# Moving every on-chip buffer of a two-block transformer kernel by 96 bytes, and packing the first block's split activations in 1,024-byte tiles

## The chip, the cores and the metric

The kernel runs on one NeuronCore of one Trainium2 chip. The metric is the device time of one execution in microseconds. TensorE (PE) multiplies, VectorE (DVE), ScalarE (ACT) and GpSimd (POOL) do the elementwise work, and DMA queues, nearly all of them issued by SyncE (SP), bring the weights from HBM.

## The reference

Two transformer blocks in float32, one after the other, on 256 tokens of width 2048 (the second one with 16 further meta tokens, so 272 positions). Each block is: norm, a wide input projection, two kinds of attention, an output projection, a residual, a norm, a gated MLP with 5632 hidden columns, a residual.

```
h = rms_norm(x, g_attn_pre) * (1 + scale_a) + shift_a
proj = h @ w_in                                   # 2048 x 5456
mixed = concat(diff_out, dsa_out) @ w_o           # 2048 x 2048
x = x + gate_a * rms_norm(mixed, g_attn_post)
h = rms_norm(x, g_ffn_pre) * (1 + scale_f) + shift_f
ff = (silu(h @ w_gate) * (h @ w_up)) @ w_down     # 2048 x 5632, twice, and 5632 x 2048
x = x + gate_f * rms_norm(ff, g_ffn_post)
# second block, 272 positions: h @ w_in_2 (2048 x 3904), attention, @ w_out_2,
# conv_glu: (silu(conv3(h @ w_gate)) * (h @ w_up)) @ w_down, same sizes
```

## The kernel before

Activations lie transposed on the chip: a tile has 128 channels on the partitions and the positions along the free dimension, so 16 tiles hold the width of 2048. The matmul takes its operands as `float32r` (one pass over the columns, with reduced precision), and the kernel wins the precision back by splitting both operands into a high and a low part. The weights arrive by DMA in `raw` (four slots of 128 x 2048 values, 1 MB each: 4 row tiles of 512 columns). ACT rounds a slot into `w_hi` (line 933), DVE subtracts that from the raw values into `w_lo` (line 1456); there are two buffers of each. PE then issues, for each of 4 output tiles and each of 4 row tiles, three matmuls: high by high, low by high, high by low.

```
pe.matmul(out, wh[:, k, c], hi(k0 + k), start=a0, stop=False)            # line 2108
pe.matmul(out, wh[:, k, c], lo(k0 + k), start=False, stop=False)         # line 2109
ins = pe.matmul(out, wl_[:, k, c], hi(k0 + k), start=False, stop=z)      # line 2110
```

The first operand is the stationary one (128 x 128 weights, loaded by a LDWEIGHTS of its own beside the matmul before), the second one moves (128 partitions by so many positions). One slot of weights gives 48 such matmuls. The order of the work is written out by hand in each engine's program and kept by semaphores.

The moving operands come from two pairs of buffers. `x_hi` and `x_lo` hold the split activations of width 2048, 16 tiles each. They are declared for 272 positions, so a tile takes 4 x 272 = 1,088 bytes of a partition, and the first block, which has 256 positions, uses the first 1,024 bytes of each. `hid_hi` and `hid_lo` hold the split hidden activations of the MLP, 44 tiles of 256 positions, 1,024 bytes each. The stretches with these matmuls, as the profile has them:

- 44 to 322 us: first block's input projection, 43 units of 48 and 36 matmuls (`x_hi`, `x_lo`, 256 positions), together 2,064
- 432 to 533: output projection, 768 (256 positions)
- 562 to 1076: gate and up projections, 4,224 (256 positions)
- 1076 to 1320: down projection, 2,112 (`hid_hi`, `hid_lo`)
- 1358 to 1830: second block's projections, 1,776 with 272 positions, 768 with 258
- 1830 to 2340: gate with 258 positions, 2,112, and up with 256 positions, 2,112, from the tiles of 1,088 bytes
- 2340 to 2602: down projection, 2,112 (`hid_hi`, `hid_lo`)

Every buffer has a fixed address, given out by `place` in the order of the declarations, each rounded up to 32 bytes, from a first address of 2208. 2208 is 160 more than a multiple of 256. The buffers that lie ahead of the constants (`raw`, `w_hi`, `w_lo`, `x_res`, `x_hi`, `x_lo`, and the arena with `hid_hi` and `hid_lo`) all have sizes that are multiples of 1,024 bytes, so before the change each of them begins 160 bytes past a multiple of 256. Within `w_hi` and `w_lo` the row tiles are 2,048 bytes apart and the column tiles 512 bytes. Only in the last unit of each quarter of the first input projection are the row tiles 336 columns, 1,344 bytes, apart.

Of the kernel before, what the change touches and what calls it, by code (L numbers as in the profile page):

```python
# [22 lines left out]
F32R = mybir.dt.float32r  # L23
# [4 lines left out]
P = 128  # L28
D = 2048
KT = D // P  # L30
# [127 lines left out]
def in1_width(n):  # L158

    return PROJ1 - 10 * COLS if ORDER_IN1[n] == 10 else COLS  # L160
# [69 lines left out]
def program(nc, a):  # L230
    with ExitStack() as ctx:
# [1 line left out]
            return ctx.enter_context(nc.semaphore(name))  # L233


        cursor = [2208]

        def place(name, shape, dt=F32, at=None):
            size = 4 * int(np.prod(shape[1:]))
            if at is None:  # L240
                at, cursor[0] = cursor[0], (cursor[0] + size + 31) // 32 * 32
            return nc.alloc_sbuf_tensor_at(name, shape, dt, offset=at)
# [14 lines left out]
        x_hi = place("x_hi", [P, KT, N2], F32R)  # L257
        x_lo_at = cursor[0]
        x_lo = place("x_lo", [P, KT, N2], F32R)
        branch_f = place("branch_f", [P, KT, S], at=x_hi_at)  # L260
        xmeta = place("xmeta", [META, D], at=x_lo_at)
        arena = cursor[0]
# [178 lines left out]
        def one(rows=P):  # L441
# [8 lines left out]
        kpe = proj2[0:64, T2_KPE, :]  # L450
        kpg = proj2[0:64, T2_CQ, :]
        norm("attn_pre", S, D, [[x_res[:, t, 0:S] for t in range(KT)]],
             [(0, x_res[:, t, 0:S], gain[:, 0, t:t + 1], x_hi[:, t, 0:S], x_lo[:, t, 0:S],
               mod[:, SH_A + t:SH_A + t + 1]) for t in range(KT)], True, given=x_sum)
        norm("diff", S, P, [[dout[:, h, :]] for h in range(8)],
             [(h, dout[:, h, :], lamv[:, 7:8], x_hi[:, h, 0:S], x_lo[:, h, 0:S], None) for h in range(8)], True)
        norm("attn_post", S, D, [[branch_a[:, t, :] for t in range(KT)]],
             [(0, branch_a[:, t, :], gain[:, 1, t:t + 1], branch_a[:, t, :]) for t in range(KT)], False,
             branch_a_ssq, direct=4)
        norm("ffn_pre", S, D, [[x_res[:, t, 0:S] for t in range(KT)]],  # L460
             [(0, x_res[:, t, 0:S], gain[:, 0, t:t + 1], x_hi[:, t, 0:S], x_lo[:, t, 0:S],
               mod[:, SH_F + t:SH_F + t + 1]) for t in range(KT)], True, column=True)
        norm("ffn_post", S, D, [[branch_f[:, t, :] for t in range(KT)]],
             [(0, branch_f[:, t, :], gain[:, 1, t:t + 1], branch_f[:, t, :]) for t in range(KT)], False,
# [32 lines left out]
        def out_bank(g):  # L497

            if g < 8:
                return bank[3]  # L500
            return bank[1 if g % 2 else 3] if g < 16 else bank[4 * (g % 2) + 3]
# [417 lines left out]
        def _(act):  # L919
# [245 lines left out]
            def take_out(g):  # L1165
                act.wait_ge(h_out, g + 1)
                b, h = out_bank(g), g % 8
                dst, src = {"diff": (dout[:, h, :], b[:, 0:S]), "dsa": (x_hi[:, 8 + h, 0:S], b[:, 0:S]),
                            "na": (na_out[:, h, 0:S], b[:, S:2 * S]),
                            "mla": (mla_out[:, h, 0:S], b[:, S:2 * S])}[kind(g)]  # L1170
                act.activation(dst, src, ACT.Copy).then_inc(h_taken, 1)
# [276 lines left out]
        def _(dve):  # L1448
# [326 lines left out]
            def take_low(g):  # L1775
                if kind(g) != "dsa":
                    return
                h = g - 8
                dve.wait_ge(h_taken, g + 1)
                dve.tensor_tensor(x_lo[:, 8 + h, 0:S], out_bank(g)[:, 0:S], x_hi[:, 8 + h, 0:S],  # L1780
                                  ALU.subtract).then_inc(h_low, 1)

            def heads(g0, g1, lead=None):
# [285 lines left out]
        def _(pe):  # L2069
# [11 lines left out]
            def dense(units, rows, hi, lo, n, cols=None, width=COLS, step=1, last_unit=True, base=0, ready=None,  # L2081
                      bank7=None, tile_ready=None, bank_ready=None, banks=None, lag=4):


                cols = cols or [P * m for m in range(len(rows))]
                for j, (k0, nk) in enumerate(units):
                    ps = d.at % SPLIT
                    if ready:
                        ready(j)
                    pe.wait_ge(raw_free[ur.at % RAW], ur.rounds())  # L2090
                    wh, wl_ = (w[ps][:, 0:nk * width].rearrange("p (k c) -> p k c", k=nk) for w in (w_hi, w_lo))
                    for m, r in enumerate(rows):
                        if j == 0:
                            free, c_ = (up_freed, up) if base else (bank_freed, t)
                            if lag == 4 or t.at + m >= lag:
                                pe.wait_ge(free, c_.value(m + 5 - lag))
                            if bank_ready:
                                bank_ready(m)
                            if bank7 is not None and m == 3:
                                pe.wait_ge(ada_copied, bank7)  # L2100
                        c = slice(cols[m], cols[m] + r)
                        out = (banks(m) if banks else bank[base + m])[0:r, 0:n]
                        for k in range(nk):
                            a0 = j == 0 and k == 0
                            if tile_ready and m == 0:
                                pe.wait_ge(n_lo, norms[tile_ready]["first"]["split"] + 4 * j + k + 1)
                            z = j == len(units) - 1 and k == nk - 1
                            pe.matmul(out, wh[:, k, c], hi(k0 + k), start=a0, stop=False)  # L2108
                            pe.matmul(out, wh[:, k, c], lo(k0 + k), start=False, stop=False)  # L2109
                            ins = pe.matmul(out, wl_[:, k, c], hi(k0 + k), start=False, stop=z)  # L2110
                        if j == len(units) - 1:
                            ins.then_inc(tile_done, 1 if m < len(rows) - 1 else 5 - len(rows))
                    if j < len(units) - 1:
                        ins.then_inc(split_used, 1)
                    if last_unit or j < len(units) - 1:
                        d.at += 1
                        ur.at += step(j) if callable(step) else step
                if base:
                    up.at += 4
                else:  # L2120
                    t.at += 4
# [2 lines left out]
                return (lambda k: x_hi[:, k, 0:n]), (lambda k: x_lo[:, k, 0:n])  # L2124


            pe.wait_ge(const_in, 16)
            pe.wait_ge(vec0_in, 48)
            pe.wait_ge(cleared, 1)
# [192 lines left out]
            for u in range(44):  # L2322
                part, n = divmod(u, 11)
                if u == 0:
                    pe.wait_ge(tile_done, 4)
                    pe.wait_ge(bank_freed, 4)
                if n == 0 and part:
                    pe.wait_ge(n_lo, norms["attn_pre"]["first"]["split"] + 4 * part + 4)
                if n in (0, 2, 4, 6):
                    ada_quarter(ADA_IN1 + 2 * part, n // 2)  # L2330
                ur.at = in1_unit(part, n)
                dense([K16[part]], TAIL1 if in1_width(n) < COLS else FOUR, *xs(S), S, width=in1_width(n),
                      banks=lambda m: in1_bank(u, m), lag=IN1_BANKS,
                      tile_ready=None if u else "attn_pre")
                if n == 6:
                    ada_columns(ADA_IN1 + 2 * part)
                if n == 7:
                    s = ADA_IN1 + 2 * part + 1
                    pe.wait_ge(beside_used, 4 * part + 4)
                    pe.wait_ge(ada_copied, s)  # L2340
                    for j in range(4):
                        ins = pe.matmul(bank[7][:, j:j + 1], acc_beside[:, P * j:P * j + P], one(), start=True,
                                        stop=True)
                    ins.then_inc(ada_cols, 1)
                if part == 3 and n in (5, 7, 8, 10):
                    rotate_rows({5: 0, 7: 1, 8: 2, 10: 3}[n])
                if u == 23:
                    pe.wait_ge(vec_in, 16 * VEC_LOADS)
                    for j in range(3):
                        ins = pe.transpose(bank[6][:, P * j:P * j + P], packs[:, 1 + j, :], ident)  # L2350
                    ins.then_inc(packs_turned, 1)
# [209 lines left out]
                    pe.wait_ge(n_lo, norms["diff"]["first"]["split"] + 4 * (j - 1))  # L2561

            def out1(i, ready=None, bank_ready=None):
                dense(K_O, FOUR, *xs(S), S, step=2, ready=ready, bank_ready=bank_ready)
                ada_sum(i + ADA_OUT1)
            pe.wait_ge(ada_copied, ADA_OUT1)
            ur.at = UNIT_OUT1
# [19 lines left out]
            spread("ffn_pre")  # L2587

            def mlp1(i, tile_ready=None, ada_block=None):
                dense(K16, FOUR, *xs(S), S, tile_ready=tile_ready,  # L2590
                      step=2 if ada_block is not None else (lambda j: 9 if j == 0 else 1) if tile_ready else 1)
                if ada_block is not None:
                    pe.wait_ge(up_freed, up.value(4))
                    ada_sum(ada_block, bank[7])
                dense(K16, FOUR, *xs(S), S, base=4, bank7=None if ada_block is None else ada_block + 1)
            mlp1(0, "ffn_pre")
            loop(4, (8, 4, 12, 4), lambda i: mlp1(i + 1, ada_block=i + ADA_MLP1))
            loop(6, (8, 4, 8, 4), lambda i: mlp1(i + 5))
# [209 lines left out]
```

## Time and profile before

| | |
|---|---|
| median of 3 runs | 2601.63 us (2600.87 to 2602.52) |
| profiled execution, first to last instruction | 2602.4 us |
| PE busy | 2494.1 us (96%), 20,022 matmuls |
| DVE, ACT, POOL busy | 1441.4, 1033.4, 292.1 us |
| DMA | 504 MB, 57% of the 16 engines' span in the main queue |

"Busy" of PE counts overlapping matmuls, each some 0.28 us long, while a new one starts every 0.12 us; so the pace is read from the starts, or from how many there are in a window. In a window's count stand also those that had begun ahead of it. Idle time of an engine is put down to what released it. The profile's own execution differs from the median of the runs by less than 1 us.

### The profile page before, as it was taken

The page shows a single profiled execution, that of the slowest core. Times are in us where ns is not written, and L with a number is a line of the kernel's source. Part 1 is how long each engine was busy: PE and PEld are TensorE (multiplying, and loading weights), DVE is VectorE, ACT ScalarE, POOL GpSimd, SP SyncE. Part 2 cuts the span into 40 slices and gives each one's busy share as a digit, 9 for nine tenths or more (in the row PEclk, how much of TensorE's full clock was granted, in tenths as well). Part 3 has the DMA queues.
Part 4 walks back from the last instruction along what each step waited for, and adds up shares of the span by engine and source line. Part 5 has one row for each costly group of instructions (what it writes and reads, how often), then busy time and mean ns, then how long its engine had stood idle before and what let it go on. Part 6 is the DMA issues. An engine that isn't in the chain of part 4 may idle for free.

```text
span 2602.4 us, 47889 instructions
## 1 busy us (share of the span) xinstructions
PE 2494.1 (96%) x20022; PEld 2363.1 (91%) x20022; DVE 1441.4 (55%) x1926; ACT 1033.4 (40%) x1332; POOL 292.1 (11%) x372
## 2 busy tenths in 40 slices
PE   6999988989999999999989998998999999999999
PEld 4999847969999999999979997778999999999999
DVE  3677657965674444433455555655655555554443
ACT  3533244344333343333334336443444444443333
POOL 5000122410100000011113002113000000000000
PEclk8999989989999999999989999999999999999999
DMA  9887864977786555555544442313455555555553
GB/s 343 288 285 269 288 210 171 333 270 236 246 289 198 179 186 184 176 180 186 179 137 154 141 152 65 125 65 130 146 179 188 181 177 180 179 189 178 179 180 127
DMA packets 263862, 504.24 MB, mean 194 GB/s; under 512 B 17152, under 2 KB 26283, under 8 KB 263467
## 3 DMA queue, kind: packets, MB, share of 16 engines
q1 hardware_dynamic: 257899, 494.97, 56.9%
q10 hardware_dynamic: 5840, 7.52, 0.9%
q8 instruction: 91, 1.49, 0.2%
q14 instruction: 32, 0.26, 0.0%
HBM read 498.04 MB, written 2.10 MB: 192 GB/s over the span
## 4 chain that ended last, share of the span: by engine, by line
PE 78%; DVE 8%; ACT 4%; issue 4%; DMA 3%; SPq 1%; ACTq 1%; POOL 1%; DVEq 0%; POOLq 0%
PE bank L2108 24%; PE bank L2110 23%; PE bank L2109 23%; ACT w_hi L933 3%; DVE w_lo L1456 3%; PE bank L2143 1%; DMA raw<-in_w_in 1%; DVE ada_acc L1484 1%; DVE tmp L1590 1%; DMA staged<-in_w_ada 1%; SPq L644 1%; PE bank L2252 1%; SPq L737 1%; PE bank L2453 0%; ACTq L1065 0%
## 5 line engine op out<-in xcount | busy, mean ns | idle before, releaser
L1456 DVE TENSOR_TENSOR w_lo<-raw,w_hi 128x2048 fp32r<-128x2048 f32 (+3 forms) x386 | 862.9, 2236 | 954.0 <-ACT w_hi L933 953.6
L2108 PE MATMUL bank<-x_hi,w_hi 128*128 128x256 f32 (+2 forms) x4608 | 1320.8, 287 | 33.7 <-DVE w_lo L1456 19.1
L2109 PE MATMUL bank<-x_lo,w_hi 128*128 128x256 f32 (+2 forms) x4608 | 1308.3, 284 | 0.0
L2110 PE MATMUL bank<-x_hi,w_lo 128*128 128x256 f32 (+2 forms) x4608 | 1307.7, 284 | 0.0
L933 ACT ACTIVATE w_hi<-raw 128x2048 fp32r<-128x2048 f32 (+3 forms) x386 | 718.9, 1862 | 1043.6 <-PE bank L2110 916.5
L2108 PEld LDWEIGHTS bank<-x_hi,w_hi 128*128 128x128 f32 x4608 | 874.2, 190 | 70.0 <-issue 39.7
L2110 PEld LDWEIGHTS bank<-x_hi,w_lo 128*128 128x128 f32 x4608 | 876.1, 190 | 0.0
L2109 PEld LDWEIGHTS bank<-x_lo,w_hi 128*128 128x128 f32 x4608 | 872.3, 189 | 1.2 <-issue 1.2
L2108 PE MATMUL bank<-hid_hi,w_hi 128*128 128x256 f32 x1408 | 399.6, 284 | 2.2 <-DVE x_res L2004 1.1
L2110 PE MATMUL bank<-hid_hi,w_lo 128*128 128x256 f32 x1408 | 398.4, 283 | 0.0
L2109 PE MATMUL bank<-hid_lo,w_hi 128*128 128x256 f32 x1408 | 398.4, 283 | 0.0
L2108 PEld LDWEIGHTS bank<-hid_hi,w_hi 128*128 128x128 f32 x1408 | 270.2, 192 | 3.6 <-issue 1.9
L2109 PEld LDWEIGHTS bank<-hid_lo,w_hi 128*128 128x128 f32 x1408 | 270.2, 192 | 0.0
L2110 PEld LDWEIGHTS bank<-hid_hi,w_lo 128*128 128x128 f32 x1408 | 270.2, 192 | 0.0
L798 POOL TENSOR_TENSOR hid_lo<-gpad,hid_hi 128x256 f32 x88 | 60.5, 719 | 1002.0 <-ACT hid_hi L1418 503.0
L1484 DVE SCALAR_TENSOR_TENSOR ada_acc<-raw,csilu,ada_acc 128x512 f32<-128x512 f32 x120 | 96.9, 807 | 3.9 <-DMA raw<-in_w_ada 0.5
L1658 DVE TENSOR_TENSOR proj<-proj,bank 128x256 f32<-128x256 f32 (+1 forms) x129 | 47.1, 415 | 10.0 <-PE bank L2110 9.9
L2143 PE MATMUL bank<-raw,csilu 128*32 128x512 f32 x320 | 47.0, 673 | 5.4 <-DMA raw<-in_w_ada 3.2
L1044 ACT ACTIVATE x_hi<-tmp 128x258 fp32r<-128x258 f32 (+2 forms) x56 | 23.4, 424 | 67.4 <-DVE tmp L1590 67.4
L1624 DVE SCALAR_TENSOR_TENSOR acc_beside<-beside,csilu,acc_beside 128x512 f32<-128x512 f32 x60 | 46.7, 778 | 2.9 <-DMA beside<-in_w_ada 1.8
L776 POOL TENSOR_TENSOR branch_f_ssq<-branch_f 128x256 f32 x12 | 16.0, 1330 | 170.0 <-ACT branch_f L1214 168.2
L1414 ACT ACTIVATE gpad<-tmp 128x256 f32<-128x256 f32 x44 | 17.8, 405 | 37.6 <-DVE tmp L2045 37.6
(332 smaller groups left out, 1458.4 us busy)
## 6 DMA issues: line engine op xcount, KB each, us to landing
raw<-in_w_gate SPq DMA_DIRECT2D x88, 1024.0 KB, 5.2
raw<-in_w_up SPq DMA_DIRECT2D x88, 1024.0 KB, 5.2
raw<-in_w_ada SPq DMA_DIRECT2D x72, 1024.0 KB, 6.6
raw<-in_w_in SPq DMA_DIRECT2D x68, 1024.0 KB, 5.7
raw<-in_w_down SPq DMA_DIRECT2D x64, 1024.0 KB, 5.0
raw<-in_w_down SPq DMA_DIRECT2D x32, 768.0 KB, 4.3
beside<-in_w_ada SPq DMA_DIRECT2D x16, 1024.0 KB, 7.7
raw<-in_w_o SPq DMA_DIRECT2D x16, 1024.0 KB, 6.3
```

The costliest lines, as they stand in the source:

```text
L644: sp.dma_start(staged[4 * s + q][:, :].rearrange("p (k c) -> p k c", k=nk), src).then_inc(staged_in[4 * s + q], 16)
L737: sp.dma_start(bias_raw[64 * half:64 * half + 64, h, :, :], src).then_inc(bias_in, 16)
L798: pool.tensor_tensor(lo, gpad[:, m, 0:S], hi, ALU.subtract).then_inc(hid_low, 1)
L933: act.activation(w_hi[ps][:, 0:width], raw[slot][:, 0:width], ACT.Copy).then_inc(hi_ready, 1)
L1456: dve.tensor_tensor(w_lo[ps][:, 0:width], raw[slot][:, 0:width], w_hi[ps][:, 0:width], ALU.subtract).then_inc(raw_free[slot], 1)
L1484: ins = dve.scalar_tensor_tensor(ada_acc[:, :], w, s, ada_acc[:, :], ALU.mult, ALU.add)
L1624: ins = dve.scalar_tensor_tensor(acc_beside[:, :], w, c_, acc_beside[:, :], ALU.mult, ALU.add)
L1658: dve.tensor_tensor(t_, t_, in1_bank(u, m)[0:rows, 0:S], ALU.add).then_inc(bank_freed, 2 if tail and m == 2 else 1)
L2108: pe.matmul(out, wh[:, k, c], hi(k0 + k), start=a0, stop=False)
L2109: pe.matmul(out, wh[:, k, c], lo(k0 + k), start=False, stop=False)
L2110: ins = pe.matmul(out, wl_[:, k, c], hi(k0 + k), start=False, stop=z)
L2143: ins = pe.matmul(ada_bank(s)[32 * k:32 * k + 32, :], csilu[:, 4 * q + k:4 * q + k + 1].broadcast_to([P, 32]), w[:, k * COLS:(k + 1) * COL ...
```

## The change

The first address becomes 2304, which is 9 x 256. All other addresses follow, 96 bytes later, so the same buffers now begin at multiples of 256. Two further names, `x1_hi` and `x1_lo`, are laid over `x_hi` and `x_lo` with tiles of 256 positions, 1,024 bytes apart, and everything in the first block that wrote or read the first 256 positions of `x_hi` and `x_lo` goes by them. The second block keeps its tiles of 1,088 bytes. No instruction is added, removed or moved on any engine; sizes, waits and queues stay as they were.

```diff
-        cursor = [2208]
+        cursor = [2304]
...
         x_lo = place("x_lo", [P, KT, N2], F32R)
+        x1_hi = place("x1_hi", [P, KT, S], F32R, at=x_hi_at)
+        x1_lo = place("x1_lo", [P, KT, S], F32R, at=x_lo_at)
...
         norm("attn_pre", S, D, [[x_res[:, t, 0:S] for t in range(KT)]],
-             [(0, x_res[:, t, 0:S], gain[:, 0, t:t + 1], x_hi[:, t, 0:S], x_lo[:, t, 0:S],
+             [(0, x_res[:, t, 0:S], gain[:, 0, t:t + 1], x1_hi[:, t, :], x1_lo[:, t, :],
                mod[:, SH_A + t:SH_A + t + 1]) for t in range(KT)], True, given=x_sum)
...
-                dst, src = {"diff": (dout[:, h, :], b[:, 0:S]), "dsa": (x_hi[:, 8 + h, 0:S], b[:, 0:S]),
+                dst, src = {"diff": (dout[:, h, :], b[:, 0:S]), "dsa": (x1_hi[:, 8 + h, :], b[:, 0:S]),
...
+            x1 = (lambda k: x1_hi[:, k, :]), (lambda k: x1_lo[:, k, :])
...
-                dense([K16[part]], TAIL1 if in1_width(n) < COLS else FOUR, *xs(S), S, width=in1_width(n),
+                dense([K16[part]], TAIL1 if in1_width(n) < COLS else FOUR, *x1, S, width=in1_width(n),
...
-                dense(K_O, FOUR, *xs(S), S, step=2, ready=ready, bank_ready=bank_ready)
+                dense(K_O, FOUR, *x1, S, step=2, ready=ready, bank_ready=bank_ready)
...
-                dense(K16, FOUR, *xs(S), S, base=4, bank7=None if ada_block is None else ada_block + 1)
+                dense(K16, FOUR, *x1, S, base=4, bank7=None if ada_block is None else ada_block + 1)
```

The other norms of the first block ("diff" and "ffn_pre"), the low halves of the sparse heads and the first call of the gate projection are changed in the same way.

## Rows read from the trace of the kernel before

**Rows 1.** The page's busy times: busy us, share, instructions.

```profile
PE 2494.1 (96%) x20022; PEld 2363.1 (91%) x20022; DVE 1441.4 (55%) x1926; ACT 1033.4 (40%) x1332; POOL 292.1 (11%) x372
```

**Rows 2.** The page's chain that ended last, by engine.

```profile
PE 78%; DVE 8%; ACT 4%; issue 4%; DMA 3%; SPq 1%; ACTq 1%; POOL 1%; DVEq 0%; POOLq 0%
```

**Rows 3.** Groups of PE by shape: busy us, mean ns; idle before, releasers.

```profile
L2108 PE MATMUL bank<-x_hi,w_hi 128*128 128x256 f32 x3040 | 863.1, 284 | 20.9 <-DVE w_lo L1456 15.3 <-DVE x_lo L1578 5.1
L2108 PE MATMUL bank<-hid_hi,w_hi 128*128 128x256 f32 x1408 | 399.6, 284 | 2.2 <-DVE x_res L2004 1.1 <-DVE w_lo L1456 0.9
L2108 PE MATMUL bank<-x_hi,w_hi 128*128 128x258 f32 x960 | 276.4, 288 | 8.9 <-DVE x_lo L1576 4.0 <-DVE w_lo L1456 3.7 <-DVE x_res L2004 0.9
L2108 PE MATMUL bank<-x_hi,w_hi 128*128 128x272 f32 x544 | 163.1, 300 | 3.9 <-DVE x_lo L1576 2.9 <-ACT proj L1361 1.0
L2108 PE MATMUL bank<-x_hi,w_hi 128*64 128x272 f32 x48 | 13.8, 288 | 0.0
L2108 PE MATMUL bank<-x_hi,w_hi 128*80 128x256 f32 x16 | 4.4, 278 | 0.0
```

**Rows 4.** Windows of dense matmuls: length, busy us (count) by engine, clock, DMA.

```profile
1150.00:1198.00 48.00, 48.00 (x402) 48.00 (x401) 18.55 (x9) 15.50 (x9) 0.00 (x0) 1.00 0.49 167
950.00:998.00 48.00, 48.00 (x408) 47.98 (x407) 19.76 (x12) 19.26 (x17) 2.63 (x4) 1.00 0.58 181
1776.00:1812.00 36.00, 36.00 (x303) 36.00 (x302) 18.80 (x19) 12.30 (x7) 21.24 (x25) 1.00 0.53 173
1444.00:1459.00 15.00, 15.00 (x121) 15.00 (x120) 11.71 (x15) 5.14 (x7) 0.00 (x0) 1.00 0.45 141
```

**Rows 5.** Timeline of PE in attention: start us, us, instruction.

```profile
1592.12 0.27 PE L2458 MATMUL bank<-cst,sheets 128*128 128x128 f32 x1
1592.23 0.27 PE L2459 MATMUL bank<-cst,sheets 128*128 128x128 f32 x1
...
1592.45 0.60 PE L2480 MATMUL bank<-turned,vtok 128*128 128x256 f32 x2
1592.88 0.59 PE L2481 MATMUL bank<-turned,vtok 128*128 128x256 f32 x2
```

**Rows 6.** Timeline of PE, last unit of a quarter, weight tiles 1,344 bytes apart.

```profile
115.39 0.28 PE L2108 MATMUL bank<-x_hi,w_hi 128*128 128x256 f32 x1
115.51 0.27 PE L2109 MATMUL bank<-x_lo,w_hi 128*128 128x256 f32 x1
...
116.79 0.28 PE L2108 MATMUL bank<-x_hi,w_hi 128*128 128x256 f32 x1
```

**Rows 7.** Windows: first block's first quarter; start of the kernel.

```profile
44.00:113.00 69.00, 68.57 (x549) 65.10 (x550) 44.10 (x45) 39.44 (x65) 12.24 (x11) 0.95 0.82 292
252.00:322.00 70.00, 67.23 (x536) 62.42 (x533) 50.70 (x70) 19.12 (x13) 11.65 (x8) 0.98 0.85 286
...
0.00:18.00 18.00, 5.96 (x25) 2.30 (x25) 0.29 (x1) 3.37 (x4) 1.10 (x12) 1.00 0.91 333
18.00:36.00 18.00, 12.21 (x77) 6.84 (x76) 4.57 (x15) 7.36 (x14) 16.17 (x25) 1.00 1.03 375
```

**Rows 8.** The two halves of the weight split, from the page's costliest groups.

```profile
L1456 DVE TENSOR_TENSOR w_lo<-raw,w_hi 128x2048 fp32r<-128x2048 f32 (+3 forms) x386 | 862.9, 2236 | 954.0 <-ACT w_hi L933 953.6
...
L933 ACT ACTIVATE w_hi<-raw 128x2048 fp32r<-128x2048 f32 (+3 forms) x386 | 718.9, 1862 | 1043.6 <-PE bank L2110 916.5
```

More of the change, by code:

```diff
@@ L452, in program @@
         norm("attn_pre", S, D, [[x_res[:, t, 0:S] for t in range(KT)]],
-             [(0, x_res[:, t, 0:S], gain[:, 0, t:t + 1], x_hi[:, t, 0:S], x_lo[:, t, 0:S],
+             [(0, x_res[:, t, 0:S], gain[:, 0, t:t + 1], x1_hi[:, t, :], x1_lo[:, t, :],
                mod[:, SH_A + t:SH_A + t + 1]) for t in range(KT)], True, given=x_sum)
         norm("diff", S, P, [[dout[:, h, :]] for h in range(8)],
-             [(h, dout[:, h, :], lamv[:, 7:8], x_hi[:, h, 0:S], x_lo[:, h, 0:S], None) for h in range(8)], True)
+             [(h, dout[:, h, :], lamv[:, 7:8], x1_hi[:, h, :], x1_lo[:, h, :], None) for h in range(8)], True)
         norm("attn_post", S, D, [[branch_a[:, t, :] for t in range(KT)]],
@@ L460, in program @@
         norm("ffn_pre", S, D, [[x_res[:, t, 0:S] for t in range(KT)]],
-             [(0, x_res[:, t, 0:S], gain[:, 0, t:t + 1], x_hi[:, t, 0:S], x_lo[:, t, 0:S],
+             [(0, x_res[:, t, 0:S], gain[:, 0, t:t + 1], x1_hi[:, t, :], x1_lo[:, t, :],
                mod[:, SH_F + t:SH_F + t + 1]) for t in range(KT)], True, column=True)
@@ L1779, in take_low @@
                 dve.wait_ge(h_taken, g + 1)
-                dve.tensor_tensor(x_lo[:, 8 + h, 0:S], out_bank(g)[:, 0:S], x_hi[:, 8 + h, 0:S],
+                dve.tensor_tensor(x1_lo[:, 8 + h, :], out_bank(g)[:, 0:S], x1_hi[:, 8 + h, :],
                                   ALU.subtract).then_inc(h_low, 1)
@@ L2589, in mlp1 @@
             def mlp1(i, tile_ready=None, ada_block=None):
-                dense(K16, FOUR, *xs(S), S, tile_ready=tile_ready,
+                dense(K16, FOUR, *x1, S, tile_ready=tile_ready,
                       step=2 if ada_block is not None else (lambda j: 9 if j == 0 else 1) if tile_ready else 1)
```

## The prediction, made before the changed kernel was run

> **What bounds the kernel now.** I read the page's busy times first. PE is busy for 96% of the span, DVE for 55%, ACT for 40% [rows 1], and the chain that ended last lies on PE for 78% of the span, on DMA for 3% [rows 2]. So the kernel is paced by the starts of the matmuls, and what the change can do must show as another distance between two starts. The groups by shape say how many there are: of the first row of each triple 3,040 + 16 with 256 positions from `x`, 1,408 from `hid`, 960 with 258, 544 + 48 with 272 [rows 3]. Times three that is 9,168, 4,224, 2,880 and 1,776, together 18,048 of the 20,022 matmuls. Of the 9,168, the program gives 7,056 to the first block and 2,112 to the second block's up projection. PE idles ahead of the largest group for only 20.9 us [rows 3].
>
> The pace comes from windows of nothing but such matmuls at a granted clock of 1.00, which is 2.4 GHz. A matmul is 0.28 us long and starts 0.12 us after the one before, so two of each count began ahead of the window. From `hid`: 402 - 2 in 48 us, 120.0 ns. From `x` with 256 positions: 408 - 2 in 48 us, 118.2 ns. With 258 positions: 301 in 36 us, 119.6 ns. With 272: 119 in 15 us, 126.1 ns [rows 4]. 256 columns at 2.4 GHz are 106.7 ns, so each matmul pays 11.5 to 13.3 ns more than its columns.
>
> Is that the price of changing weights for every matmul? The attention says no. Its plain float32 matmuls, each with weights of its own too, start 0.11 us apart with 128 columns, and four of them with 256 columns (two rows of two) take 2 x 0.43 us, 0.217 us each [rows 5]. These are two passes over the columns (106.7 and 213.3 ns) plus about 3 ns. They want a value every second cycle, the dense ones want one every cycle. The extra 9 to 10 ns stand only where the values are wanted at full rate: a matter of supply from on-chip memory, where addresses can count.
>
> And addresses do count. `hid` and `x` have the same shape and clock but 120.0 against 118.2 ns [rows 4]; what differs is the distance of tiles, 1,024 against 1,088 bytes. In the last unit of a quarter, where the weight tiles too step by 64 bytes past a multiple of 256, twelve matmuls go from 115.39 to 116.79 us, 116.7 ns each [rows 6], and it repeats every three matmuls, though from triple to triple both addresses move by 64 bytes. So moving both operands by 64 bytes changes nothing; how they stand to each other, modulo 256, does. What no row shows is an operand at any other place modulo 64 than 32: 2208 leaves 32, and all sizes and steps here are multiples of 64.
>
> **The change part by part.** No instruction, wait or queue changes, so there are four terms: the pace of the dense matmuls by family, and the DMA.
>
> For the pace at multiples of 64 there is no row, so I bound it. The lower end is the excess of the float32 matmuls, 3 ns over the columns [rows 5]: 109.3 ns for 256 columns. The upper end is the worst family, `hid` with 120.0 [rows 4], and above it no more than some ns for a clash that whole pieces could make longer. Between them I take a mechanism. If the values are fetched in pieces of 64 bytes (16 values, 6.7 ns at one a cycle), a tile that starts 32 past a multiple of 64 spans 17 pieces for 1,024 bytes, an aligned one 16. The piece saved is worth 16 columns: 126.1 - 118.2 = 7.9 ns for 16 further columns with 272 against 256 positions [rows 4], of which I take the 6.7.
>
> - `hid`, 4,224 matmuls: 120.0 to 113.3 ns, 28.3 us.
> - First block's `x1`, 7,056: now they have the tile distance of `hid`, so I give them its new pace: 118.2 to 113.3, 34.6 us.
> - 272 positions, 1,776: 1,088 bytes span 18 pieces before and 17 after, 6.7 ns each, 11.9 us.
> - 258 positions, 2,880: 1,032 bytes span 17 pieces before and after, 0.
> - Up projection of the second block, 2,112, starts at 0, 64, 128 or 192 modulo 256: as the first block's, 10.3 us.
>
> Together 85.1 us. What is late next? A unit of 48 matmuls would take 5.4 us instead of 5.7. The split of the next weights takes 1.86 us on ACT and then 2.24 on DVE [rows 8], 4.1 us, with two buffers: still covered, by 1.3 us. The DMA is the tighter one in the first input projection, at a share of 0.82 to 0.85 and 286 to 292 GB/s, while the start of the kernel shows that 375 can be had [rows 7]. There I keep only half of 2,064 x 4.9 = 10.1 us, which takes 5 off. The sum is 80 us.
>
> The DMA itself also gets other destinations. No row shows a transfer to another alignment. The bounds are nothing and, from the spread between two saturated stretches (333 and 375 GB/s, 11% [rows 7]), 11% of the 3% of the chain that is DMA [rows 2], 9 us of 78. I take the nearer end, nothing. The Trainium skill, "DMA: Bandwidth & Descriptors", section How a descriptor splits into AXI transactions, has a rule here: bytes between the 256-byte boundary below and a descriptor's start still cost beats. For 2,048 bytes that begin 160 past one, it would make 69 beats of 64, an estimate of 7% or 5 us on the 78; no run here shows it.
>
> Against the profiled execution of 2602.4 us (the median of the runs is 2601.6): 2602.4 - 80 = **2522 us**.
>
> **The rivals.** *Only the distance counts (slower).* If moving everything by 96 bytes changes no more than the 64 of rows 6 do, then `hid`, the second block and the weights stay as they are, and the first block takes over the distance and with it the pace of `hid`: 7,056 x (120.0 - 118.2) = 12.7 us, 2615 us. For it: it rests on a measured family alone, and on the indifference to 64 bytes. Against it: nothing but that 32 modulo 64 was never varied. It decides if `hid` is still at 120.0. The Trainium skill speaks for this one, in "SBUF — State Buffer", section Specifications (TRN2): cachelines of 16 bytes, with a penalty for each change of line. 160 and 0 are both whole lines, so by that rule the shift is void and the sum would be this rival's.
>
> *The excess goes altogether.* 109.3 ns for 256 columns, 110.2 for 258, 116 for 272: 62.8 + 45.2 + 19 + 27 + 18 = 172 us, of which the DMA in the first input projection (287 x 118.2 / 109.3 = 310 GB/s) and the split take back about 12: 2442 us. For it: the float32 matmuls have no excess at all. The Trainium skill, "TensorE: Matmul & The Clock Gate", section Back-to-back issue gap, lists 262 cycles for 256 columns; that is 109.2 ns, this rival's pace. Against it: the unit of rows 6 gets to 116.7 at the same alignment, so clashes between the two streams exist besides, and the second block's 1,088 stay.
>
> *A small gain.* Alignment shifts the clashes a little, `hid` to 117, the first block with it: 4,224 x 3 + 7,056 x 1.2 = 21 us, 2581 us.
>
> *Nothing to be measured.* A gain in `hid` pays for the loss in the first block: within 5 us.
>
> *A longer clash.* Weights and moving values now start on the same whole piece together, so the later one waits 6.7 rather than 3.3 ns: 18,048 x 2 to 3 ns, 2640 to 2655 us. Nothing in the rows asks for it, nothing excludes it.
>
> **How the numbers follow.** Forecast (2500 to 2550) 0.32; only the distance 0.22; excess gone 0.15; small gain 0.12; nothing 0.11; longer clash 0.08. Faster by over 0.2% (5.2 us, about what a measurement of this kernel can tell from no change) is 0.32 + 0.15 + 0.12 = 0.59, the same 0.11, slower 0.30. The forecast's own range is 2500 to 2550. For 8 in 10 I leave out the longer clash and the lower part of "excess gone": 2445 to 2622.
>
> **What would show it.** In windows of the same stretches after: `hid` at 113 ns (some 425 matmuls in 48 us) for the forecast, 120.0 for "only the distance", 109 for "excess gone". The first block must equal `hid` in every case; if it doesn't, the distance of tiles is not what told them apart. The second block's 258 positions stay at 119.6 in the forecast and fall to 110 if the excess goes. ACT's and DVE's mean of 1862 and 2236 ns should stay. If PE's idle time behind `w_lo` grows from 15.3 us to over 40, the split was nearer than I think. The prediction is wrong if `hid` moves by less than 2 ns.

## The result, and the profile after

The changed kernel took 2608.76 us (median of 20 runs) where the kernel before took 2601.78 (20 runs): a ratio of 1.0022, 95% interval 1.0014 to 1.0030, so 5.7 us slower by the ratio (3.6 to 7.8); the medians differ by 7.0. One execution of the 20, at a granted clock of 0.84 for 0.98, took 2723.94 and is left out of the ratio. The forecast of 2522 us was wrong, in sign too. The rival "only the distance counts" has the mechanism; its 12.7 us are about twice what came.

The page of the kernel after, busy times and chain by engine, for [rows 1] and [rows 2]:

```profile
PE 2503.6 (96%) x20022; PEld 2373.2 (91%) x20022; DVE 1437.9 (55%) x1926; ACT 1032.7 (40%) x1332; POOL 285.9 (11%) x372
```

```profile
PE 80%; DVE 8%; ACT 4%; issue 4%; DMA 2%; SPq 1%; POOL 1%; DVEq 0%; ACTq 0%; POOLq 0%
```

Same instructions. PE was busy 9.5 us longer and its weight loads 10.1 us; DVE, ACT and POOL were busy 3.5, 0.7 and 6.2 us less. The profiled execution grew from 2602.4 to 2608.9 us. The pace shows where. The same windows as in [rows 4], of the kernel after (length, busy us and count of PE, PEld, DVE, ACT, POOL; granted clock; DMA share; GB/s), first `x` in the first block, then `hid`:

```profile
950.00:998.00 48.00, 48.00 (x403) 48.00 (x402) 20.16 (x13) 19.60 (x17) 2.64 (x4) 1.00 0.58 182
1150.00:1198.00 48.00, 48.00 (x402) 48.00 (x401) 19.29 (x9) 14.71 (x9) 3.97 (x3) 1.00 0.48 159
```

Less the two that began ahead, `x` has 401 starts in 48 us where [rows 4] had 406, and `hid` has 400 in both. A window's count is good to one start. The paces below are finer: the distance of starts, worked out over every uninterrupted run of twelve or more of one kind. The first block's gate and up projections went from 118.31 to 119.96 ns, its input projection from 118.11 to 119.76. `hid` has 119.97 before and after, the second block's up projection 118.15 and 118.15, 258 positions 119.75 and 119.76, 272 positions 125.97 and 126.05.

The groups by shape of the kernel after (busy us, mean ns; idle before, releasers), for [rows 3], and the split's two halves, for [rows 8]:

```profile
L2110 PE MATMUL bank<-x_hi,w_hi 128*128 128x256 f32 x3040 | 868.4, 286 | 20.5 <-DVE w_lo L1458 14.8 <-DVE x_lo L1580 5.4
L2110 PE MATMUL bank<-hid_hi,w_hi 128*128 128x256 f32 x1408 | 399.6, 284 | 2.2 <-DVE x_res L2006 1.1 <-DVE w_lo L1458 0.9
L2110 PE MATMUL bank<-x_hi,w_hi 128*128 128x258 f32 x960 | 276.3, 288 | 9.0 <-DVE x_lo L1578 4.0 <-DVE w_lo L1458 3.8 <-DVE x_res L2006 0.9
```

```profile
L1458 DVE TENSOR_TENSOR w_lo<-raw,w_hi 128x2048 fp32r<-128x2048 f32 (+3 forms) x386 | 862.0, 2233 | 959.6 <-ACT w_hi L935 959.5
...
L935 ACT ACTIVATE w_hi<-raw 128x2048 fp32r<-128x2048 f32 (+3 forms) x386 | 718.3, 1861 | 1043.5 <-PE bank L2112 941.4
```

Of these only the group that holds the first block's `x` grew, 5.3 us on its third of the matmuls; `hid` and 258 positions stood still, and the mean durations of the split on ACT and DVE moved by 1 and 3 ns.

**Where the time stands.** From the first dense matmul to the first of `hid` it is 44.3 to 1076.3 us before and 43.6 to 1081.8 after, so 6.2 us more. From there on the two traces run alike (about 1,521 us to `hid`'s last). Within the first block, the gate and up stretch took 5.0 us more. Its distances of up to 135 ns between starts sum to 495.2 before and 502.7 after (+7.5), the longer ones, which hold waits, to 20.7 and 18.1 (-2.6); the profile lays 1.0 of that to waits for `w_lo` (3.7 to 2.7 us). The input projection took 2.1 more (+3.1 short, -1.4 long, the rest uncounted), the output projection 0.8. The attention between them varies by some us with the kernel: 99.4 us before, 97.9 after, 94.0 to 98.3 in other runs of this study.

Of the DMA no effect can be seen on the path: its share of the chain went from 3% to 2%, and did so too in the run with the distance alone (experiment 3). Main queue, and issue to landing of the gate's pieces, after:

```profile
q1 hardware_dynamic: 257899, 494.97, 56.4%
```

```profile
raw<-in_w_gate SPq DMA_DIRECT2D x88, 1024.0 KB, 5.1
```

It was 56.9% and 5.2 us before; pieces of `w_in` went from 5.7 to 5.4 us, those of `w_o` from 6.3 to 6.9. In the profiles of the whole kernel, pieces of `w_in` took 5.3 and 5.4 us at the first address of 2304 and 5.5 to 5.7 at 2208, too small a difference, and off the path, to build on.

### The profile page after: what moved, and what is told of

The parts are those of the page before. It is cut to its first block, busy times and chain, and to the rows that moved or that the text cites. A ratio compares the mean times of both kernels' runs of the same rounds, so it can differ in the third digit from the quotient of the medians.

```text
span 2608.9 us, 47889 instructions
## 1 busy us (share of the span) xinstructions
PE 2503.6 (96%) x20022; PEld 2373.2 (91%) x20022; DVE 1437.9 (55%) x1926; ACT 1032.7 (40%) x1332; POOL 285.9 (11%) x372
## 4 chain that ended last, share of the span: by engine, by line
PE 80%; DVE 8%; ACT 4%; issue 4%; DMA 2%; SPq 1%; POOL 1%; DVEq 0%; ACTq 0%; POOLq 0%
PE bank L2110 25%; PE bank L2111 24%; PE bank L2112 24%; ACT w_hi L935 3%; DVE w_lo L1458 3%; PE bank L2147 1%; DMA raw<-in_w_in 1%; DVE tmp L1592 1%; DVE ada_acc L1486 1%; SPq L646 1%; DMA staged<-in_w_ada 1%; PE bank L2256 1%; SPq L739 1%; PE bank L2457 0%; POOL diag L863 0%
## 5 line engine op out<-in xcount | busy, mean ns | idle before, releaser
L1458 DVE TENSOR_TENSOR w_lo<-raw,w_hi 128x2048 fp32r<-128x2048 f32 (+3 forms) x386 | 862.0, 2233 | 959.6 <-ACT w_hi L935 959.5
L935 ACT ACTIVATE w_hi<-raw 128x2048 fp32r<-128x2048 f32 (+3 forms) x386 | 718.3, 1861 | 1043.5 <-PE bank L2112 941.4
```

What stands on the lines that cost most here:

```text
L935: act.activation(w_hi[ps][:, 0:width], raw[slot][:, 0:width], ACT.Copy).then_inc(hi_ready, 1)
L1458: dve.tensor_tensor(w_lo[ps][:, 0:width], raw[slot][:, 0:width], w_hi[ps][:, 0:width], ALU.subtract).then_inc(raw_free[slot], 1)
```

## The experiments

**1. The matmuls by themselves.** The forecast stood on an alignment to 64 that no row showed. I used a small kernel with the dense triple alone (high weights with high values, high with low, low with high), in segments of 96 matmuls that differ in one address each. One line of its list, `W` and `M` being multiples of 256:

```
# name, weights at, step, to low half, moving at, step, to low half, columns, weight columns
("rel32", W, 2048, 16384, M + 32, 1024, 32768, 256, 128)
```

> A kernel with nothing but the disputed matmuls: it computes nothing of the reference and leaves all other engines idle while PE runs 37 segments of 8 x 12 matmuls in the order high by high, low by high, high by low, each segment with its own addresses for the 128 x 128 weights and the 256 moving columns. Theory 1 (only the place of the moving values against the weights modulo 256 counts): the segments 'same0' to 'same224', both operands moved together, all pace at 120 ns as `hid` does; 'rel16' to 'rel240' differ from one another, some at 117 or less; 'step64' 118.2 and 'both64' 116 to 117. Theory 2 (whole pieces of 64 bytes count, but something in the kernel hid it): 'same0', 'same64', 'same128' at 113 and 'same32', 'same96', 'same160' at 120. If the excess comes from the other engines' use of the memory, all segments fall to 109.

Windows of eight us in six of its segments (same columns as above): both at 0; both at 32; both at 16; moving values 32 past the weights; weight tiles and moving tiles both 64 further from each other; 64 weight columns.

```profile
76.00:84.00 8.00, 8.00 (x69) 8.00 (x68) 0.00 (x0) 0.00 (x0) 0.00 (x0) 1.00 0.00 0
99.00:107.00 8.00, 8.00 (x69) 8.00 (x68) 0.00 (x0) 0.00 (x0) 0.00 (x0) 1.00 0.01 2
88.00:96.00 8.00, 8.00 (x70) 8.00 (x69) 0.00 (x0) 0.00 (x0) 0.00 (x0) 1.00 0.01 2
183.00:191.00 8.00, 8.00 (x71) 8.00 (x70) 0.00 (x0) 0.00 (x0) 0.00 (x0) 1.00 0.00 0
350.00:358.00 8.00, 8.00 (x71) 8.00 (x70) 0.00 (x0) 0.00 (x0) 0.00 (x0) 1.00 0.00 0
422.00:430.00 8.00, 8.00 (x73) 8.00 (x72) 0.00 (x0) 0.00 (x0) 0.00 (x0) 1.00 0.00 0
```

With every other engine and the DMA idle, the excess over the columns is all there. The paces of each segment, without its first twelve matmuls, ns:

| both operands at | 0, 32, 64, 96, 128, 160, 224 | 16 |
|---|---|---|
| | 120.00 each | 118.30 |

| moving minus weights | 16 | 32 | 48 | 64 | 96 | 128 | 160 | 192 | 224 | 240 | 256, 512, 1024 |
|---|---|---|---|---|---|---|---|---|---|---|---|
| | 118.66 | 116.63 | 118.31 | 117.77 | 120.04 | 118.65 | 118.69 | 117.77 | 118.31 | 117.16 | 120.0 |

With tiles 1,024 apart, where both stand makes no difference in steps of 32 bytes; how far the one is past the other, modulo 256, does. The kernels' own paces come out: `hid`'s 120.0 with moving tiles 1,024 apart, `x`'s 118.33 with 1,088, and 116.12 where the weight tiles have the extra 64 bytes as well, for the 116.7 of [rows 6]. This last case needs a closer look: the weights and the values of each matmul are at distance 0 there, exactly as with `hid`, and still it is 4 ns faster. What is no longer at 0 is the weights of the next row tile, which are loaded while the values of the last one still move. So the distance of the two operands of one matmul doesn't tell the pace by itself; that the loads beside it are what counts fits, but no segment took it apart. The excess belongs to the matmul and hardly to its length: 258 columns 119.7, 272 126.1, 288 131.7, 512 226.7 ns, that is 12.2, 12.8, 11.7 and 13.3 over 107.5, 113.3, 120.0 and 213.3.

Fewer weight columns change the pace too, but not simply for the better. With both operands at 0, 64 weight columns instead of 128 halve the excess, 113.34 ns, while 32 give 117.8. The kernel of experiment 6 has 64 columns at four more distances: with the moving values 32, 64, 128 and 192 past the weights 119.1, 116.7, 116.7 and 119.1 ns, where 128 columns have 116.6, 117.8, 118.7 and 117.8 in the table. Windows of 32 columns at 0, and of 64 columns at 32:

```profile
432.00:440.00 8.00, 8.00 (x70) 7.33 (x68) 0.00 (x0) 0.00 (x0) 0.00 (x0) 1.00 0.00 0
1736.00:1744.00 8.00, 8.00 (x69) 8.00 (x68) 0.00 (x0) 0.00 (x0) 0.00 (x0) 1.00 0.01 2
```

So both the place of the weights and their number of columns count, which puts the loading of the weights among the causes. That less of it is always better is refuted. Plain float32 takes 215.8 for two passes, as in [rows 5].

**2 and 3. The change in its two parts.** The shift alone, and the distance alone:

```diff
# shift only, on the kernel before         # distance only, on the kernel after
-        cursor = [2208]                   -        cursor = [2304]
+        cursor = [2304]                   +        cursor = [2208]
```

> The kernel before with the first address 2304 and its tiles of 1,088 bytes kept. Theory 1: nothing changes, 2601.8 us within 2, x at 118.2 ns and hid at 120.0. Theory 2, that a gain by the shift pays for part of the loss by the tiles: 2596 to 2600 us.

> The changed kernel with its first address back at 2208, so only the first block's tiles are 1,024 bytes apart. Theory 1: all of the loss, 2607 to 2609 us, the first block at 119.6 to 120.0 ns, as in the changed kernel. Theory 2: more than the changed kernel's loss, 2610 us or above.

The same two windows, shift only:

```profile
950.00:998.00 48.00, 48.00 (x408) 47.98 (x407) 20.97 (x13) 18.14 (x16) 2.63 (x4) 1.00 0.55 175
1150.00:1198.00 48.00, 48.00 (x402) 48.00 (x401) 18.50 (x9) 16.00 (x10) 0.00 (x0) 1.00 0.52 176
```

and distance only:

```profile
950.00:998.00 48.00, 48.00 (x403) 48.00 (x402) 20.82 (x13) 18.11 (x16) 2.64 (x4) 1.00 0.57 182
1150.00:1198.00 48.00, 48.00 (x402) 48.00 (x401) 18.77 (x9) 15.95 (x9) 1.35 (x2) 1.00 0.50 173
```

The shift alone: 2601.04 against 2603.31 us, ratio 0.9994 (0.9983 to 1.0005), counts in both windows as in [rows 4] to the last matmul. The distance alone: 2610.54, ratio 1.0033 (1.0019 to 1.0047), counts as in the kernel after. That is 8.6 us of loss (4.9 to 12.2) for the distance alone, against 5.7 (3.6 to 7.8) for the whole change: the intervals overlap, and the paces are the same. So the tiles of 1,024 bytes carry the loss, and the shift, with all that it does to the DMA's destinations, is worth between 4.4 us less and 1.3 us more. Within these bounds the second theory, that the shift gives a little back, is not excluded: the median of 2610.54 lies in its range, though the kernel before also took 1.5 us more beside these runs than beside the changed kernel.

**4. Which distances are good.** The same small kernel with 217 segments: the moving values at eight distances past the weights, each with the low half of one operand, of the other or of both moved as well, and then tiles of 1,056 and 1,088 bytes, also with 258 and 272 columns.

> The disputed matmuls alone again (it computes nothing of the reference), with 217 segments at other distances. r is how far the moving tiles lie past the weights modulo 256, m a further shift of the low moving tiles, w one of the low weights, b one of both; then tiles 1,056 and 1,088 bytes apart, and 258 and 272 columns. Theory 1 (the distance between the two streams modulo 256 sets the pace): r0 120.0, r32 116.6, r64 117.8, r96 120.0, r128 118.7 again; b keeps high with high and low with low at their distance, so r0_b stays near 120; no segment under 113. The rival, that steps between tiles count more than the distance: r0_p1056 and r0_p1088 at 118.2 whatever r is.

Most of the grid lies between 117 and 120 ns, the worst at 121.2. One place stands out: moving values 192 and low weights 128 past the high weights, 113.3 ns. I had expected that with no distance between the operands, moving both low halves together would keep 120; it gave 117.0 to 117.9 for six of seven moves, and 120.0 only for 192 bytes. With tiles of 1,088 bytes the rival in the expectation nearly came true: 118.3 ns at the four distances that are multiples of 64 and 118.9 at the other four, wherever the first tile stands. With 1,056 bytes it did not (116.7 to 118.9). And one pair that had 118.65 in experiment 1 (128 apart) had 120.0 here, another (160) went from 118.7 to 117.3, at the very same addresses. So the pace is not a function of these addresses alone. The segment ahead, and the one of the eight result banks at which a segment begins, were others; neither was varied by itself.

**5. A first use: 32 bytes between the operands.** On the kernel after (code cut):

```diff
-        cursor = [2304]
+        cursor = [2208]
 ...
+        cursor[0] += 32        # ahead of x_res, and so of x and hid; the weights lie below
```

> The changed kernel with its first address back at 2208 and 32 unused bytes ahead of x_res, so every moving operand lies 32 bytes further from the weights. Theory 1: x1 and hid at 116.6 ns, as the segment rel32 paced. First block 7,056 x (120.0 - 116.6) = 24 us and hid 4,224 x 3.4 = 14 us less than the changed kernel: 2608.8 - 38 = 2571 us, some 1.2% under the kernel before. If the distance to the weights doesn't carry over from the small kernel to this one: 2607 to 2609 us.

The two windows:

```profile
950.00:998.00 48.00, 48.00 (x410) 47.95 (x409) 22.05 (x13) 19.18 (x20) 2.63 (x4) 1.00 0.57 185
1150.00:1198.00 48.00, 47.83 (x406) 47.63 (x406) 20.57 (x10) 16.95 (x13) 6.49 (x5) 1.00 0.53 180
```

2581.48 against 2602.72 us, ratio 0.9920 (0.9907 to 0.9933). `hid` fell to 117.1 ns, `x` in the first block to 116.8 to 117.0, close to the small kernel's 116.6. The expectation was 2571. Of the 10 us that were missing, the paces explain some 4, chiefly `hid` in the first block (117.49) and the second block's up projection, which became slower (118.88). The waits behind `w_lo` and `x_lo` are 0.9 us longer than in the kernel after; the rest stays open.

**6. The best place, at several common addresses, and the 1,088-byte tiles there.**

> The disputed matmuls alone (it computes nothing of the reference), 148 segments: tiles 1,088 bytes apart with 256, 258 and 272 columns at four distances r of the moving tiles and eight shifts w of the low weights; tiles 1,024 apart around r192 with w128; and that point at three common addresses. Theory 1 (distances modulo 256 set the pace, deterministically): best256, best32 and best160 all at 113.3 ns again. If the one 113.3 seen was chance: one of them at 117 or more. With 1,088 bytes all between 117 and 120 for 256 columns, since the distance changes from tile to tile.

The best pair at two common addresses, 0 and 32:

```profile
1660.00:1672.00 12.00, 12.00 (x109) 12.00 (x107) 0.00 (x0) 0.00 (x0) 0.00 (x0) 1.00 0.00 1
1680.00:1692.00 12.00, 12.00 (x108) 12.00 (x107) 0.00 (x0) 0.00 (x0) 0.00 (x0) 1.00 0.01 1
```

113.33 and 113.33 ns (and 113.35 at 160): the common address again has no part. It is a narrow place: 32 bytes away the segments have 117.0 to 118.9, and with the low moving values 128 bytes further 121.2. With tiles of 1,088 bytes the same pair gives only 119.3 to 119.5 for 256 columns, and 258 columns reach up to 121.8. (The kernel has 141 segments, where the expectation says 148.)

**7 and 8. The best place in the kernel**, once with the first block's tiles of 1,024 bytes, once with the 1,088 of the kernel before:

```diff
# 7: on the kernel after, with cursor = [2208]; 8: on the kernel before (cut at ...)
+        cursor[0] += 128       # ahead of w_lo
 ...
+        cursor[0] += 64        # ahead of x_res: x and hid are now 192 past w_hi
```

> The changed kernel with its first address back at 2208, 128 unused bytes ahead of w_lo and 64 more ahead of x_res: the low weights then lie 128 bytes and all moving operands 192 bytes past the high weights, modulo 256. Theory 1: x1 and hid at 113.3 ns. Against the kernel before 7,056 x (118.2 - 113.3) = 34.6 us and 4,224 x (120.0 - 113.3) = 28.3 us, less some 8 us that PE then waits longer for the split weights: 2602 - 55 = 2547 us. If other engines' accesses disturb so tight a pattern: x1 and hid at 117 to 118, 2580 to 2595 us.

> The kernel before, tiles of 1,088 bytes in both blocks, with the same 128 and 64 unused bytes ahead of w_lo and x_res. Theory 1, with the paces of the small kernel: hid 120.0 to 113.4 (4,224 x 6.6 = 28 us less), the first block 118.2 to 119.4 (7,056 x 1.2 = 8.5 us more), 258 columns 119.7 to 121.5 (2,880 x 1.8 = 5 us more), the second block's up projection 118.2 to 119.4 (2.5 us more), 272 columns 0.8 us less: 2602 - 13 = 2589 us. If the unused bytes alone make the gain, whatever the tiles are: 2559 us.

Windows of experiment 7:

```profile
950.00:998.00 48.00, 47.95 (x422) 47.75 (x421) 21.28 (x13) 19.53 (x17) 2.63 (x4) 1.00 0.58 184
1150.00:1198.00 48.00, 47.67 (x421) 47.48 (x420) 19.71 (x10) 19.28 (x14) 8.88 (x8) 1.00 0.59 206
```

and of experiment 8:

```profile
950.00:998.00 48.00, 48.00 (x404) 48.00 (x403) 19.91 (x13) 18.56 (x17) 2.62 (x4) 1.00 0.53 179
1150.00:1198.00 48.00, 48.00 (x426) 48.00 (x426) 18.74 (x10) 17.74 (x12) 0.00 (x0) 1.00 0.54 187
```

| pace, ns | before | after | 7: pads, 1,024 | 8: pads, 1,088 |
|---|---|---|---|---|
| `hid` | 119.97 | 119.97 | 113.44 | 113.43 |
| `x`, first block, gate and up | 118.31 | 119.96 | 113.49 | 119.38 |
| `x`, first block, input projection | 118.11 | 119.76 | 113.97 | 119.12 |
| up projection, second block | 118.15 | 118.15 | 119.43 | 119.43 |
| 258 positions | 119.75 | 119.76 | 121.54 | 121.53 |
| 272 positions | 125.97 | 126.05 | 125.58 | 125.55 |

Experiment 7 took 2558.87 against 2602.16 us, ratio 0.9839 (0.9823 to 0.9854); experiment 8 2587.84 against 2601.86, ratio 0.9948 (0.9935 to 0.9960). Number 7 is the best version of the study and beats both kernels; number 8 came within 1.2 us of its expected 2589. The tiles of 1,024 bytes, a loss of 0.3% by themselves, are worth 29 us beside the pads. Number 7 missed its expectation of 2547 by 12 us: 258 positions took back 2,880 x 1.8 ns = 5.2 us, the up projection 2,112 x 1.3 = 2.7, and the first block's input and output projections stayed at 114.0 and 114.1 ns, some 2 us. The distances over 135 ns in the first block's dense stretches and in both down projections grew by 10 us together, where 8 had been allowed for all longer waits. The waits of PE behind the split weights (us in total, times, longest), before and in experiment 7:

```profile
PE bank L2108 <- DVE w_lo L1456: 20.0, 26, 3.3
```

```profile
PE bank L2112 <- DVE w_lo L1460: 25.6, 31, 3.5
```

## Why the prediction was wrong, step by step

- **The bound.** Right: PE's distance of starts sets the time, and where it moved the span moved, though by less than starts times nanoseconds.
- **The excess is a matter of addresses, not of changing weights.** Right, and now shown apart: at one shape and one sequence of weights the small kernel gives 113.3 to 121.2 ns by addresses alone, with no other engine at work. This also refutes my reading that the values' own stream is short of supply. The values alone would have given the same at every distance from the weights. My reading of [rows 6] was only half right, too: there both operands of each matmul stand at distance 0, as with `hid`, and the pace is 116.7 for 120.0. "How they stand to each other" therefore can't mean the two operands of one matmul alone.
- **Pieces of 64 bytes.** This is the step that failed: "a tile that starts 32 past a multiple of 64 spans 17 pieces ... an aligned one 16". `hid` was to go from 120.0 to 113.3; it has 119.97 before, after, and with the shift alone. In the small kernel 32, 96 and 160 give the same 120.00 as 0, 64 and 128. [rows 6] had already said that a common shift of 64 changes nothing; the honest reading was to expect the same of 96, and I put an unmeasured mechanism in its place. Through this step `hid` (28.3 us), the first block (34.6), 272 positions (11.9) and the second block's up projection (10.3) all entered the sum, and none of them gained anything. That the gap of 6.7 ns reappears with the best distance is a coincidence of size, or a common unit below both; nothing here tells which.
- **The Trainium skill's rule.** I had weighed "SBUF — State Buffer", Specifications (TRN2), in the Trainium skill: cachelines of 16 bytes, and a penalty for each change of line. From it I took that a shift of whole lines is void. The shift of 96 bytes was (0.9994). A shift of both by 16 bytes was not: 118.30 ns against 120.00. So the rule pointed the right way, and does not describe what happens at one line's step.
- **The first block equals `hid`.** Right: 119.96 and 119.97 ns, "in every case", which made it a useful anchor. The loss is 7,056 x 1.65 = 11.6 us by it.
- **The rival's 12.7 us, against 5.7 in the runs (3.6 to 7.8).** Its pace was rounded up, 1.8 for 1.65. Of the 11.6 us, the short distances show 7.5 in gate and up and 3.1 in the input projection. Some 4 us come back at the long ones (-2.6 and -1.4): a slower PE waits less for what is prepared beside it. The profile's waits for `w_lo` show 2.1 of these (3.7 to 2.7 us in gate and up, 4.2 to 3.1 in the input projection); that the rest has the same cause is argued, no run took it apart. The rest lies within what one profiled execution differs from another, the attention's 94 to 99 us for example. The price of the rival was thus mis-sized mainly because it took every added nanosecond for time on the path.
- **258 and 272 positions, second block.** 258 stayed, as forecast. 272 was to give 11.9 us and the up projection 10.3; both gave nothing, by the same failed step.
- **ACT and DVE** stayed: 1861 and 2233 ns for 1862 and 2236. The cover of the split was never tested by the change; experiment 7, at `hid` and `x` of 113.4 to 114.1 ns, tests it: 5.6 us more waiting for `w_lo`, 2.4 of them in the input projection, 1.6 in the output projection and 1.8 in gate and up. So "covered, by 1.3 us" held in the main, not at the places where PE waited already.
- **The DMA** taken as nothing: right within what the shift alone leaves (-4.4 to +1.3 us). The estimate of 5 us from "DMA: Bandwidth & Descriptors" in the Trainium skill, How a descriptor splits into AXI transactions, would lie just outside. That section speaks of bytes that are fetched, and what moved here was where they land, so the run doesn't test it on its own ground. (69 beats for 64, on 78 us, would be nearer 6 us than 5.)
- **The chances.** 0.22 for "only the distance" was too little: it was the one case whose pace and whose indifference both had rows. The forecast itself, the small gain and the longer clash rested on paces that no row showed, and had 0.52 among them.

What stays open is why the distance counts. Reads of weights and values that meet in the same part of memory would fit the period of 256, the excess per matmul that is nearly constant, and the 116.1 ns where only the weights loaded beside a matmul stand elsewhere. It doesn't explain by itself why 32 weight columns are slower than 64, and 64 at a distance of 32 slower than 128. Different paces at the same addresses would fit two streams that lock into one of several rhythms. Neither was shown, and the bank that the results go to, a rival, was not varied by itself.

## What to carry to other kernels

Where matmuls are paced by their starts, work out that distance to a tenth of a ns for each pair of tiles, and compare it with columns over clock. If the excess differs between tiles of one shape, the relative address of weights and moving values, those of neighbouring matmuls included, is a knob. Try it in a small kernel with the matmuls alone, since the paces found there came back in the whole kernel (120.0 as 119.97, 113.3 as 113.4 to 114.1, 116.6 as 116.7 to 117.5), and set pads by it, for every width in use. Then price them by a run: of the nanoseconds per matmul, only a part showed in the time, as the waits moved the other way (5.7 us of 11.6 here). And where a row already shows that a change of one kind is void, the forecast should begin from that row, not from a mechanism that would exempt the next case.

## What the runs showed that I had not expected

- Aligning everything to 256 bytes changes neither the pace of the matmuls nor the time by anything that can be measured (0.9994); a pad of 128 and one of 64 bytes, with tiles of 1,024, take 1.6%.
- The best distance (low weights +128, moving values +192) gives 113.3 ns; with the low moving values 128 bytes further it is 121.2.
- Fewer weight columns can be slower: 64 of them at a distance of 32 bytes 119.1 ns, 128 of them 116.6.
- The best distance is best only with tiles 1,024 apart. At 1,088 the same pads make matmuls slower: 258 positions go from 119.8 to 121.5 ns, 256 from between 118.1 and 118.3 to between 119.1 and 119.4. Only 272 positions gain, 126.0 to 125.6.
- A common shift by 16 bytes gives 118.3 ns, by any multiple of 32 tried 120.0.
